# Where ScalarE's last query evictions and the choice of the second unit of experts stand in a one-core fp32 kernel with 512 gathered rows

## The reference, cut to what matters

```python
q = (t @ wq).reshape(ntok, PEER_HEADS, 2, PEER_DH)
sc = einsum('thpd,hpkd->thpk', q, subkeys)
s1, i1 = top_k(sc[:, :, 0], 16)
s2, i2 = top_k(sc[:, :, 1], 16)
cand = s1[..., :, None] + s2[..., None, :]
best, pos = top_k(cand, 16)
idx = e1 * 128 + e2                      # from i1, i2 and pos
gate = softmax(best)
act = gelu(einsum('phkd,pd->phk', u_tab[idx], t)) * gate
out = einsum('phk,phkd->pd', act, v_tab[idx])
```

## Time and profile before

| | |
|---|---|
| median of 3 runs | 4532.99 us (4530.13 to 4540.94) |
| the profiled execution | 4548.1 us, span 4546.3 us |
| first gather issued | 2761.4 us |
| first product with a gathered row on VectorE | 2803.5 us |
| first product with a gathered row on TensorE | 2844.5 us |
| last gather issued | 4523.5 us |
| PE, DVE, ACT, POOL busy | 80%, 44%, 21%, 30% of the span |
| mean DMA rate | 181 GB/s; 309 GB/s from 2845 to 3600 us, 352 GB/s from 3600 to 4510 us |

### The profile page before, as it was taken

One profiled execution on the slowest core, in us unless ns is written; L12 is line 12 of the kernel. 1 busy time (PEld: TensorE's weight loads), 2 busy tenths in 40 slices (PEclk: granted clock), 3 DMA queues, 4 the chain that ended last, 5 costly groups with the idle time before them and its releaser, 6 DMA issues.

```text
span 4546.3 us, 45133 instructions
## 1 busy us (share of the span) xinstructions
PE 3634.2 (80%) x16837; PEld 2083.1 (46%) x16837; DVE 2016.4 (44%) x4562; ACT 968.8 (21%) x2181; POOL 1363.9 (30%) x1494
## 2 busy tenths in 40 slices
PE   6788998999999779999997887877777854555455
PEld 3355534555555564444476775435444521111111
DVE  2565062632232781111144215766554555655553
ACT  3564032200000211100033221441222211112111
POOL 0000001253222000000000002654555666777776
PEclk8899999999999889999998898988789977767777
DMA  4232102222222133322221235987788998999998
GB/s 174 74 112 80 56 23 48 80 100 106 81 88 113 62 127 135 111 74 74 74 97 38 75 114 176 339 308 259 271 315 319 363 346 310 362 353 356 358 367 312
DMA packets 287763, 821.55 MB, mean 181 GB/s; under 512 B 24040, under 2 KB 60340, under 8 KB 284244
## 3 DMA queue, kind: packets, MB, share of 16 engines
q0 software_dynamic: 150832, 565.17, 33.8%
q1 hardware_dynamic: 136320, 253.22, 15.7%
q10 hardware_dynamic: 420, 0.62, 0.0%
HBM read 791.67 MB, written 27.26 MB: 180 GB/s over the span
## 4 chain that ended last, share of the span: by engine, by line
PE 59%; DVE 12%; POOL 8%; issue 8%; ACT 6%; DMA 4%; another core or an unknown queue 3%; SPq 0%; ACTq 0%; DVEq 0%; POOLq 0%
PE bank L716 24%; PE bank L2584 8%; PE bank L2817 5%; POOL arena L1158 4%; POOL ring L1149 4%; PE bank L2387 3%; PE bank L2544 2%; DVE ring L2251 2%; PE bank L2439 2%; DMA arena<-in_peer_v,arena 1%; PE bank L2303 1%; PE bank L581 1%; PE bank L2679 1%; PE bank L2379 1%
## 5 line engine op out<-in xcount | busy, mean ns | idle before, releaser
L2817 PE MATMUL bank<-arena 64*64 64x512 f32 x4096 | 671.1, 770 | 435.6 <-issue 293.9
L1149 POOL DMA_INDIRECT ring<-in_peer_u,arena x512 | 535.4, 1046 | 1263.2 <-DVE arena L2209 1071.9
L2251 DVE SCALAR_TENSOR_TENSOR ring<-ring,xT 128x1024 f32<-128x1024 f32 x512 | 616.8, 1223 | 341.2 <-DMA ring<-in_peer_u,arena 313.2
L1158 POOL DMA_INDIRECT arena<-in_peer_v,arena x512 | 578.1, 1129 | 458.3 <-PE bank L2817 295.3
L2817 PEld LDWEIGHTS bank<-arena 64*64 64x64 f32 x4096 | 184.6, 164 | 845.1 <-issue 842.2
L716 PE MATMUL bank<-hT,ring 128*128 128x512 f32 (+1 forms) x1536 | 553.3, 522 | 5.1 <-ACT hT L631 5.1
L716 PE MATMUL bank<-arena,ring 128*128 128x512 f32 (+1 forms) x1536 | 551.3, 521 | 0.0
L716 PEld LDWEIGHTS bank<-hT,ring 128*128 128x128 f32 x1536 | 292.6, 191 | 264.0 <-issue 250.9
L2584 PE MATMUL bank<-hT,ring 128*128 128x256 f32 x1536 | 365.6, 397 | 56.5 <-DVE hT L1980 22.6
L716 PEld LDWEIGHTS bank<-arena,ring 128*128 128x128 f32 x1536 | 291.8, 190 | 258.1 <-issue 244.2
L2584 PEld LDWEIGHTS bank<-hT,ring 128*128 128x128 f32 x1536 | 301.4, 199 | 135.0 <-issue 44.9
(11 more groups left out here) (516 smaller groups left out, 4548.9 us busy)
## 6 DMA issues: line engine op xcount, KB each, us to landing
ring<-in_mlp_w SPq DMA_DIRECT2D x32, 2048.0 KB, 8.4
ring<-in_ada_w SPq DMA_DIRECT2D x24, 2048.0 KB, 10.5
s_store<-arena POOLq DMA_DIRECT2D x8, 2816.0 KB, 9.6
ring<-in_w_in SPq DMA_DIRECT2D x10, 2048.0 KB, 7.9
arena<-s_store SPq DMA_DIRECT2D x16, 1024.0 KB, 6.9
ring<-in_w_in SPq DMA_DIRECT2D x12, 1024.0 KB
ring<-in_w_out SPq DMA_DIRECT2D x4, 2048.0 KB, 8.0
ring<-in_s_w_glu SPq DMA_DIRECT2D x4, 2048.0 KB, 20.7
```

The source lines that it names most:

```text
L1149: pool.indirect_dma_start(u_row[k % ERING], None, I["peer_u_2"][0], bass.IndirectOffsetOnAxis(idxs[:, k // EXPERTS, k % EXPERTS:k % EXPERT ...
L1158: pool.indirect_dma_start(v_row[v % ERING], None, I["peer_v_2"][0], bass.IndirectOffsetOnAxis(idxs[:, v // EXPERTS, v % EXPERTS:v % EXPERT ...
L2251: dve.scalar_tensor_tensor(row, row, 1.0, h_tok[k // EXPERTS % 2], ALU.mult, ALU.mult, accum_out=dots[k // ERING % 2][:, k % ERING:k % ERI ...
L2817: last = pe.matmul(banks[2 * r + n][QUADS[r if y == 0 else 1 - r], :], diag[QUADS[r], s, :], v_row[s][QUADS[r], 512 * n:512 * n + 512], st ...
```

## The change

ScalarE no longer evicts query tiles 8 to 15 ahead of `gate_exp(0)`. It does so in ticks 0 to 7, one in each, ahead of the tick's steps of half 1. Its `gate_exp(1)` goes from tick 10 to tick 14. VectorE no longer chooses unit 1 ahead of row 0. It runs `key_choice(1)` in tick 3, `pair_choice(1)` in tick 6, `expert_numbers(1)` in tick 10, each behind that tick's row and ahead of the tick's steps of half 1, and `gate_share(1)` in tick 18 in place of 12. TensorE's, POOL's and SP's programs are as they were.

```diff
+LATE_QUERIES = steps("pq", 8, 16)
...
             for step, n in side_order(0):
-                side(step, 0, n)
+                if (step, n) not in LATE_QUERIES:
+                    side(step, 0, n)
...
                 if tokens_at(k):
                     keep_tokens(tokens_at(k))
-                if k == 10:
+                if k == 14:
                     gate_exp(1)
+                if k < len(LATE_QUERIES):
+                    side("pq", 0, LATE_QUERIES[k][1])
...
             dve.wait_ge(S("peer_landed"), 32)
-            for u in range(2):
-                key_choice(u)
-                pair_choice(u)
-                expert_numbers(u)
+            key_choice(0)
+            pair_choice(0)
+            expert_numbers(0)
             gate_share(0)
...
-                if k == 12:
+                if k == 3:
+                    key_choice(1)
+                if k == 6:
+                    pair_choice(1)
+                if k == 10:
+                    expert_numbers(1)
+                if k == 18:
                     gate_share(1)
```

## The result

| | before | after |
|---|---|---|
| median of 20 executions each | 4537.4 us (4507 to 4561) | 4546.7 us (4529 to 4566) |
| ratio, 95% interval | | 1.0028 [1.0015, 1.0041], or +12.7 us [+6.8, +18.6] of 4533 |
| the profiled execution | 4548.1 us, span 4546.3 us | 4565.9 us, span 4563.8 us |
| POOL's first gather, the zero point below | 2761.37 us | 2764.21 us |
| TensorE's first gathered product (from that gather) | 83.1 us | 92.6 us |

The account below looks back on a forecast made before the run. It took TensorE's chain of waits to bound the changed passage, the DMA the stretch from 3600 us; -3.0 + 7.3 + 7.7 - 8.6 + 1.0 = +4.4 us on 4533.0 gave 4537.4 us, range 4526 to 4550 us.

Parts of the forecast that it names:

- The frame: Passage from 2761 to 2845 us: TensorE's progress to its first gathered product counts; row 0 going early is worth nothing.
- Squares: ScalarE does `msq` in ticks 2 and 3, so TensorE's wait for the squares goes: -3.0 us.
- Early gathers against the query block: Gathers issued earlier delay the last query weight block before tile 12: +7.3 us, bounds 0 and +10.9.
- `pair_choice(1)`: In tick 6, between `mscl` 0 to 3 and 4 to 7, it makes TensorE wait within `xr` 0: +7.7 us.
- Second block: Half 1's second weight block, before `xr` 2, takes 6.3 us in place of 14.9: -8.6 us, bounds -9.7 and 0.
- `expert_numbers(1)`: In tick 10, its 3.2 us on VectorE are hidden by TensorE's block wait and `xr` 2: nothing.
- Later loads: Third weight block 12 us later, 1.05 MB moved from an idle into a full DMA stretch: +1.0 us, from 0 to 2.7.
- Rows set the pace: Rival: VectorE's and POOL's progress decides at 2845 us, so the 25.2 us gap goes, less 4.6: 4512 us; 7%.
- The queue stays long: Rival: half 1's second weight block still takes 14.9 us behind gathers and small loads: +13.0 us, 4546 us; 13%.
- It evens out: Rival: later DMA-bound stretches swallow a shift of a few us, the bytes being the same: 4533 us; 12%.
- the lower clock behind a new wait: Within `xr` 0 and 1, TensorE restarts at the lower clock after the wait for `mscl` 4: 1.6 us more.

Follow-up runs that it names:

- a2: VectorE's part of the change alone (plus `gate_exp(1)` in tick 14), ScalarE evicting as before; 1.0040 against the kernel before, 4550.5 to 4532.4 us.
- e2: The changed kernel, but POOL's ninth gather waits until the last query block has landed; 0.9991 against the kernel before, 4531.7 to 4532.4 us.
- e1: The changed kernel, but all of unit 1's choice in tick 3; 1.0013 against the kernel before, 4539.6 to 4532.4 us.
- a0_again: The changed kernel once more, unaltered, for its trace; one execution, 4536.6 us to 4528.4 us for the kernel before.
- e6: The changed kernel, but `pair_choice(1)` in tick 6 behind `mscl` 4 to 7 and `lruz`; 1.0003 against the kernel before, 4530.2 to 4533.6 us.
- a1: ScalarE's part of the change alone, VectorE choosing both units before row 0 as before; 0.9984 against the kernel before, 4525.2 to 4532.4 us.
- e7: The changed kernel, but POOL's ninth gather waits for query tile 11, as the query block's issue does; one execution, 4546.8 us to 4528.4 us before.
- e3: The changed kernel with unit 1's choice in tick 3 and POOL's ninth gather behind the query block's landing; 0.9991 against before, 4527.9 to 4533.6 us.
- e4: The kernel before, but half 1's second weight block waits for query tile 15, not `xr` 1; 0.9980 against before, 4524.7 to 4533.6 us.
- e5: The e3 version, with half 1's second weight block also waiting only for query tile 15; 0.9960 against the kernel before, 4512.4 to 4533.6 us.
- e9: The kernel before with ScalarE's part alone and half 1's second weight block waiting only for query tile 15; 0.9960, 4512.5 to 4528.4 us.

## Why the prediction went as it did

**The frame held, the numbers in it did not.** The head start that counts is TensorE's at its first gathered product, not row 0's. Row 0 came 38 us earlier and the kernel got slower. That product was to come within 5 us of 2847.9, and I would be wrong if it came after 2855. It came at 2856.81; less the 2.84 us by which the first gather was late that is 2853.97, short of 2855 but outside the 5 us. The signs for single waits were missed too: the query block took 16.5 us, not 12 to 15, and the second block 8.9 us, not 5 to 7.

**Squares, -3.0.** Right: gone in after, still there in a2.

**Early gathers against the query block, +7.3.** Mechanism right (e2 removes it), size short: +8.6 in the profiled execution, +10.2 in e1 and a0_again. I had the block land when 5.4 MB had moved, at 390 GB/s. It took all that was left, 6.46 MB (18.0 us x 359 GB/s, e1). I had too much moved by then, a little of the gathers left over behind the block, and a rate too high. My upper bound, +10.9, held.

**`pair_choice(1)`, +7.7, bounds 6.1 to 8.** Mechanism right (e1, e6), and the wait, 5.9 us, near the 6.1. The part for the clock was short: 32 products took 3.75 + 7.76 = 11.5 us around the wait where they had taken 8.8, so 2.7 us and not 1.6. The +8.6 is above the upper bound: that bound was too tight.

**Second block, -8.6.** In the profiled execution this is the worst of the terms: -6.0. I let one gather lie beside the load, and it was as much as two: VectorE, held by `pair_choice(1)` and then by the filters, did row 7 at 2833.6 and row 8 at 2838.1, when `xr` 1 was about to end, so the gathers of row 7 of the second table (2836.3) and row 16 of the first (2839.6) went out within 3 us of the load's issue (2839.3). In a0_again, with the same gathers beside it, it was 7.4 us (2.2 MB at 298 GB/s in place of 236), so the gather left out is worth some 1.1 us over my 6.3, and the other 1.5 us are a lower rate in one execution, whose cause stays open. (My 6.3 was itself 0.2 too small: 5.2 us alone and 1.3 us for a gather are 6.5.) e1 and a1 show 11.8 and 11.9 us, with `xr` 1 done earlier: this term depends on the others, and I summed them as if they were apart.

**`expert_numbers(1)`, 0.** Right, hidden behind 7.0 us.

**Later loads, +1.0.** Not confirmed. Between the first gathered product and row 32 after lost 3.2 us more, and its trace puts that on the clock. Timeline of TensorE after, and of before at the same steps, and one window of each over tick 15's products and the step behind:

```profile
2864.22 4.56 PE L2621 MATMUL bank<-blk,hT 128*128 128x8 f32 x32
2868.71 3.69 PE L2826 MATMUL bank<-arena 64*64 64x512 f32 x16
2872.33 1.82 PE L2783 MATMUL bank<-arena 128*128 128x128 f32 x8
```

```profile
2851.90 3.74 PE L2612 MATMUL bank<-blk,hT 128*128 128x8 f32 x32
2855.57 1.95 PE L2817 MATMUL bank<-arena 64*64 64x512 f32 x16
2857.45 1.16 PE L2774 MATMUL bank<-arena 128*128 128x128 f32 x8
```

```profile
2868.20:2873.00 4.80, 4.80 (x22) 1.96 (x23) 2.33 (x5) 0.00 (x0) 1.59 (x3) 0.50 1.04 406
```

```profile
2855.30:2860.20 4.90, 4.90 (x37) 3.31 (x37) 2.71 (x8) 1.48 (x2) 3.17 (x4) 1.00 1.03 395
```

0.8 + 1.7 + 0.7 = 3.2 us. a0_again has the same code without that drop (1.95 us for the product), and took 49.0 us from the first gathered product to row 32, 0.2 more than before. The other runs agree: 52.0 or 52.1 us in all five with the drop that have no gaps of their own (after, a2, e2, e6, e7), 48.8 to 49.5 in the seven without it. So the drop costs 3 us, and the later loads next to nothing.

**The rivals.** *Rows set the pace*: refuted by e3, where rows 0 to 3 come 13 us earlier than in a1 and the passage is that of a1, and by e4, where row 0 comes no earlier than before and the kernel is 9 us faster. *The queue stays long*: its time, 4546 us, is the one measured, but not its mechanism, since the second block did get shorter. *It evens out*: refuted, though not by row 511 of single executions (in a0_again row 32 is 7.5 us late and row 511 is 12.9 us early). What refutes it are the ratios: in all ten versions that were executed several times, the shift of row 32 lies within the interval of the time, from -19.8 us (e5, time -18 us) to +12.7 us (after, time +12.7 us); e2 is at the edge of its interval. The shift survives, though the DMA is 95% busy on the way.

**The step that failed** is the sum. Four of its terms (the query block, the lower clock behind a new wait, the second block, tiles and `xr` 2 at the lower clock) were off in the same direction, by 1.3, 0.9, 2.6 and 1.5 us, with 2.2 us more behind the first gathered product. Which term is worst changes with the execution: in a0_again the query block is +10.2 us in place of +7.3, the second block -7.5 in place of -8.6, and the first gathered product 7.2 us late. So the two loads beside gathers, sized +7.3 and -8.6 and together -1.3 us, are what failed in both: they measured +2.6 and +2.7 us together. Each was small against its doubt, and I took each near its favourable side. A likely reason for the common direction, argued and not tested, is what they share: one more gather or one more stop of TensorE lengthens several at once.

## What to carry to other kernels

An engine that runs ahead issues its transfers earlier; ask which load they now stand in front of, and count all bytes that are queued, at the rate seen in a stretch that is as mixed. Work moved out of an idle gap lands between other work: look for the one consumer that waits for the instruction behind it, and count its restart at the lower clock as well. And look first at the longest wait on the path and the rule that causes it (here the condition for one load, 9 us for one line) before filling the gaps of an engine that is not on the path.

## What the runs showed that I had not expected

**A drop of TensorE's clock without a gap before it.** In the profiled execution after, the granted clock was 0.50 in the window above, the lower level (1.2 GHz), while TensorE was busy all through, and had been since the second block landed 20 us earlier. Just before it, TensorE did the 32 products of L2621. The same drop at the same step is in the profiled executions of after, a2, e2, e4, e6 and e7, and not in those of before, a1, e1, e3, e5, e9 and a0_again. Since after and a0_again are one kernel, it is not settled by the code alone; moving `pair_choice(1)` (e6) did not remove it. What sets it off stays open.

**A late signal.** After tile 11's last product (its modelled end is 2779.47) ScalarE began its eviction, and SP issued the query block, only at 2787.13.

```profile
2787.13 0.38 ACT L1509 ACTIVATE arena<-bank 128x256 f32<-128x256 f32 x1 [8.70 <-remote]
```

```profile
2787.13 0.37 SPq L441 DMA_DIRECT2D ring<-in_peer_wq  x1
```

VectorE, too, stood 3.1 us in this stretch with the same mark "remote", until 2785.64. In e1 and a0_again SP issued the block 15.3 us behind the first gather, without that delay, and in e6 after 17.2 us. The delay seems to have cost nothing: tile 12 started at 31.7 us in after and e6, and at 33.4 and 33.3 us in e1 and a0_again, where the block was issued earlier. That fits a landing set by the bytes queued with the block rather than by its issue, but no run isolates it. Why the signal came late was not tried either.
